# A three-block transformer in one kernel: 36 expert up groups moved under the choice and the spreading of the experts

## The reference

```python
q = (xt @ w_q).reshape(T, H, 256)
s1 = einsum('thd,hkd->thk', q[..., :128], keys1); s2 = einsum('thd,hkd->thk', q[..., 128:], keys2)
v1, i1 = top_k(s1, 16); v2, i2 = top_k(s2, 16)
cand = v1[..., :, None] + v2[..., None, :]          # 16 x 16 sums
sv, pos = top_k(cand, 16); eidx = take(i1 * 128 + i2, pos); gw = softmax(sv)
act = einsum('td,thkd->thk', xc, u_tab[eidx])
hact = gelu(act) * gc
return einsum('thk,thkd->td', hact, v_tab[eidx])
```

## Time and profile before

| | us |
|---|---|
| median of three runs (lowest, highest) | 3381.91 (3381.36, 3394.42) |
| profiled execution, its own time | 3379.55 |
| its span | 3377.8 |
| PE, DVE, ACT, POOL busy | 3076.7, 2061.3, 1342.0, 20.9 |
| PE idle before the transposes of the choice | 67.3 |

### The profile page before, as it was taken

One profiled execution on the slowest core, in us unless ns is written; L12 is line 12 of the kernel. 1 busy time (PEld: TensorE's weight loads), 2 busy tenths in 40 slices (PEclk: granted clock), 3 DMA queues, 4 the chain that ended last, 5 costly groups with the idle time before them and its releaser, 6 DMA issues.

```text
span 3377.8 us, 53195 instructions
## 1 busy us (share of the span) xinstructions
PE 3076.7 (91%) x19008; PEld 2712.4 (80%) x19008; DVE 2061.3 (61%) x3619; ACT 1342.0 (40%) x1953; POOL 20.9 (1%) x41
## 2 busy tenths in 40 slices
PE   8997699998999999999999898798926899999999
PEld 8986476898998798988898668784725799999998
DVE  5563543656557556567555636863599766666666
ACT  4332422444443434443444323331318644444443
POOL 0000000000000000000000000000000000000000
PEclk9999899999999999999999868898968999999999
DMA  7556143555554655554555314233410355555554
GB/s 246 186 161 188 56 162 119 174 184 201 184 183 131 219 185 186 184 172 143 198 184 189 124 54 140 90 100 113 155 44 0 101 187 186 187 187 188 187 187 157
DMA packets 141255, 525.50 MB, mean 156 GB/s; under 512 B 16154, under 2 KB 16154, under 8 KB 138320
## 3 DMA queue, kind: packets, MB, share of 16 engines
q1 hardware_dynamic: 134768, 490.79, 44.4%
q0 software_dynamic: 5520, 30.97, 2.8%
q10 hardware_dynamic: 848, 2.10, 0.2%
HBM read 520.65 MB, written 3.15 MB: 155 GB/s over the span
## 4 chain that ended last, share of the span: by engine, by line
PE 81%; DVE 12%; ACT 3%; DMA 2%; issue 2%; ACTq 0%; SPq 0%; DVEq 0%
PE psum L487 74%; PE psum L1464 2%; DMA ring<-wstream 2%; DVE wpair L458 1%; ACT small L1835 1%; DVE arena L2340 1%; PE psum L1033 1%; PE psum L611 1%; PE psum L1056 1%; ACT hpair L1839 1%; PE psum L1045 1%; PE psum L1449 0%; DVE xpair L666 0%; DVE arena L2540 0%; DVE arena L2454 0%
## 5 line engine op out<-in xcount | busy, mean ns | idle before, releaser
L487 PEld LDWEIGHTS psum<-xpair,wpair 128*128 128x128 f32 x11712 | 1461.7, 194 | 78.0 <-DVE wpair L458 41.0
L487 PE MATMUL psum<-xpair,wpair 128*128 128x256 f32 x11712 | 1475.5, 286 | 50.4 <-DVE wpair L458 38.2
L458 DVE TENSOR_TENSOR wpair<-ring,wpair 128x1024 fp32r<-128x1024 f32 (+1 forms) x872 | 1060.5, 1220 | 664.9 <-ACT wpair L455 662.6
L455 ACT CAST wpair<-ring 128x1024 fp32r<-128x1024 f32 (+1 forms) x872 | 908.1, 1044 | 1045.8 <-PE psum L487 913.9
L487 PE MATMUL psum<-wpair,hpair 128*128 128x512 f32 x3120 | 757.1, 391 | 3.4 <-DVE hpair L819 3.2
L487 PEld LDWEIGHTS psum<-wpair,hpair 128*128 128x128 f32 x3120 | 569.2, 188 | 113.8 <-issue 6.0
L487 PE MATMUL psum<-wpair,xpair 128*128 128x512 f32 (+3 forms) x1536 | 353.0, 391 | 15.6 <-DVE wpair L458 12.2
L487 PEld LDWEIGHTS psum<-wpair,xpair 128*128 128x128 f32 x1536 | 290.0, 195 | 76.9 <-DVE wpair L458 9.8
L796 ACT ACTIVATE small<-psum 128x256 f32<-128x256 f32 x260 | 99.9, 384 | 456.6 <-PE psum L487 456.6
L815 DVE TENSOR_TENSOR small<-small,arena 128x256 f32<-128x256 f32 x128 | 81.4, 636 | 141.6 <-ACT small L796 141.6
L611 PE MATMUL psum<-kc,arena 128*128 128x128 f32 (+1 forms) x212 | 44.2, 374 | 122.2 <-DVEq L2550 67.3
(11 more groups left out here) (305 smaller groups left out, 1617.1 us busy)
## 6 DMA issues: line engine op xcount, KB each, us to landing
ring<-wstream SPq DMA_DIRECT2D x934, 512.0 KB, 3.4
arena<-rows POOLq DMA_DIRECT2D x18, 1024.0 KB, 5.7
arena<-diag POOLq DMA_DIRECT2D x2, 1728.0 KB, 10.3
tbuf<-arena POOLq DMA_DIRECT2D x1, 2048.0 KB, 44.7
arena<-tbuf POOLq DMA_DIRECT2D x2, 1024.0 KB, 9.4
arena<-x_feat ACTq DMA_DIRECT2D x4, 256.0 KB, 8.7
res<-x_tok ACTq DMA_DIRECT2D x1, 1024.0 KB, 10.9
arena<-mem_feat POOLq DMA_DIRECT2D x1, 1024.0 KB, 5.0
```

The source lines that it names most:

```text
L455: eng.copy(hi, raw).then_inc(S("w_hi"), 1)
L458: eng.tensor_tensor(wpair[:, 1, o % PAIRS, 0:w], raw, hi.bitcast(F32), ALU.subtract)\
L487: mm = pe.matmul(out_, a[i], b[j], start=start and n == 0, stop=stop_ and last)
```

## The change

The first 24 up groups (`NA`) stand between the scores and the choice's transposes: PE makes them while DVE chooses, ACT puts their GELUs into `ga`, room taken from `wexp`. Pool makes the low halves of slots 0 to 25 of the expert stage; DVE makes none of them, and in the projection it no longer runs two slots ahead (`more=0`). Twelve more up groups (`NB`) stand in the spreading, one after every fifth round, with GELUs into a new tile `gb`, casts on ACT and halves on DVE in it. In every round DVE multiplies the 24 kept blocks' part straight from PSUM (`w_mul`), and then ACT copies the other 104 columns. The spreading is written out, not looped.

The expert blocks that are left run as 36 rounds of three (the up group of a new block, the down group of a new one and that of a kept one), then 54 rounds of two as before, and the last ones. The hidden tiles get a number of their own h, apart from the block f. ACT and DVE make the halves of round k + 1 in turn k. The stream is packed in the new order, and the scratch of the transfers that Pool issues is set to 4096 bytes, which makes room for `gb`. The feed-forward stages keep their code, with the number of slots a block written as 3.

```diff
+NA, NB = 24, 12
+N0 = NA + NB
+
+
+def peer_up(f):
+
+    return f if f <= N0 else N0 + 1 + 3 * (f - N0 - 1) if f <= 2 * N0 else 4 * N0 + 1 + 2 * (f - 2 * N0 - 1)
+
+
+def peer_down(f):
+    if f < N0:
+        return N0 + 1 + 3 * f + 2
+    if f < 2 * N0:
+        return N0 + 1 + 3 * (f - N0) + 1
+    return 2 * NKEY - 1 if f == NKEY - 1 else 4 * N0 + 1 + 2 * (f - 2 * N0) + 1
...
+        def pe_peer_up(pe, f, i=0, step=0):
+
+            s = STAGES["peer"]
+            pe.wait_ge(S("hid_act"), H0 + f - 1 + step * i)
+            slot = s.slot + peer_up(f)
+            w = weights(pe, slot, i)
+            for k in range(KD):
+                x_part(pe, k)
+                products(pe, psum[:, 4 + f % 2, 0:SEQ], part(w, slice(k * P, (k + 1) * P)),
+                         [xpair[:, a, k, :] for a in (0, 1)], k == 0, k == KD - 1,
+                         "hid_done" if k == KD - 1 else None)
+            hold(slot)
...
+        def pe_peer_down(pe, h, f, i=0, step=0):
+
+            s = STAGES["peer"]
+            slot = s.slot + peer_down(f)
+            w = weights(pe, slot, i)
+            pe.wait_ge(S("hid_out"), H0 + h + 1 + step * i)
+            for nn in range(2):
+                for t in range(NT):
+                    products(pe, bank(s.tile + nn, t), [hpair[:, a, h % 2, tt(t)] for a in (0, 1)],
+                             part(w, slice(nn * HALF, (nn + 1) * HALF)), h == 0, False,
+                             "down_done" if nn + t == 2 else None)
+            hold(slot)
+
+        def pe_peer(pe):
+
+
+            def round3(k, i=0):
+                pe_peer_up(pe, N0 + 1 + k, i, 4)
+                pe_peer_down(pe, 2 * k, N0 + k, i, 8)
+                pe_peer_down(pe, 2 * k + 1, k, i, 8)
+
+            def round2(f, i=0):
+                pe_peer_up(pe, f + 1, i, 6)
+                pe_peer_down(pe, f, f, i, 6)
+
+            pe_peer_up(pe, N0)
+            for k in range(4):
+                round3(k)
+            with pe.Fori(0, N0 // 4 - 2) as i:
+                for k in range(4, 8):
+                    round3(k, i)
+            for k in range(N0 - 4, N0):
+                round3(k)
+            with pe.Fori(0, (NKEY - 2 - 2 * N0) // 6) as i:
+                for f in range(2 * N0, 2 * N0 + 6):
+                    round2(f, i)
+            pe_peer_up(pe, NKEY - 1)
...
+        def act_peer(act, split):
+
+            o = ORDER[STAGES["peer"].slot][1]
+
+            def gelu(f, read, i=0, step=0):
+                act.wait_ge(S("hid_done"), H0 + f + 1 + step * i)
+                if read is not None:
+                    act.wait_ge(S("hid_out"), read)
+                act.activation(gated(f), psum[:, 4 + f % 2, 0:SEQ], ACT.Gelu).then_inc(S("hid_act"), 1)
+
+            def round3(k, i=0, slots=3):
+                gelu(N0 + k, H0 + 2 * (k - 2) + 1 + 8 * i if k >= 2 else None, i, 4)
+                for j in range(slots):
+                    split.one(o + N0 + 4 + 3 * k + j, i)
+
+            def round2(f, i=0, slots=2):
+                gelu(f, H0 + 2 * (f - N0 - 2) + 1 if f < 2 * N0 + 2 else H0 + f - 1 + 6 * i, i, 6)
+                for j in range(slots):
+                    split.one(o + 4 * N0 + 1 + 2 * (f + 1 - 2 * N0) + j, i)
...
+            def fresh_tile(k, h, i, wi, hi, step):
+
+                f = N0 + k
+                dve.wait_ge(S("hid_act"), H0 + f + 1 + step * i)
+                if h >= 2:
+                    dve.wait_ge(S("down_done"), D0 + h - 1 + hi * i)
+                dve.tensor_tensor(whole(h), gated(f), weight(f + step * i), ALU.mult).then_inc(S("hid_whole"), 1)
+                dve.wait_ge(S("hid_whole"), whole_count(k) + wi * i)
+                dve_halves(dve, h, whole(h), H0 + h + 1 + hi * i)
+
+            def early_tile(k, i, wi):
+
+                h = 2 * k + 1
+                if h >= 2:
+                    dve.wait_ge(S("down_done"), D0 + h - 1 + 8 * i)
+                if k < NA:
+                    src = ga[:, bass.ds(k + 4 * i, 1), :].rearrange("p o s -> p (o s)")
                 else:
-                    other = weight(f + i)
-                h = f0 + f
-                dve.tensor_tensor(whole(h), gated(h), other, ALU.mult).then_inc(S("hid_whole"), 1)
-                dve.wait_ge(S("hid_whole"), h + 1 + i)
-                dve.tensor_copy(hpair[:, 0, h % 2, :], whole(h)).then_inc(S("hid_hi"), 1)
-                dve.wait_ge(S("hid_hi"), h + 1 + i)
-                dve.tensor_tensor(hpair[:, 1, h % 2, :], whole(h), hpair[:, 0, h % 2, :].bitcast(F32), ALU.subtract)\
-                   .then_inc(S("hid_out"), 1)
-
-            loop_tiles(dve, split, name, per, step)
+                    src = whole(h)
+                    g = gb[:, bass.ds(k - NA + 4 * i, 1), :].rearrange("p o s -> p (o s)")
+                    dve.tensor_tensor(src, g, weight(k + 4 * i), ALU.mult).then_inc(S("hid_whole"), 1)
+                    dve.wait_ge(S("hid_whole"), whole_count(k) + 1 + wi * i)
+                dve_halves(dve, h, src, H0 + h + 1 + 8 * i)
...
+            def round3(k, i=0, slots=3):
+                wi = 4 if k < NA else 8
+                fresh_tile(k, 2 * k, i, wi, 8, 4)
+                early_tile(k, i, wi)
+                for j in range(slots):
+                    split.one(o + N0 + 4 + 3 * k + j, i)
...
-        wexp = region(0, SEQ, NKEY)
+        wexp = region(0, SEQ, NKEY - NA)
+        ga = region(SEQ * (NKEY - NA), NA, SEQ)
...
+            split.at = ORDER[STAGES["peer"].slot][1]
+            pool.wait_ge(S("w_lo"), split.at)
+            split.to(split.at + NA + 2)
...
+            for f in range(NA):
+                pe_peer_up(pe, f)
             pe.wait_ge(S("selected"), 1)
             pe_transpose(pe, "peer", [[sel[:, a, t, :] for a in (0, 1) for t in range(NT)],
                                       [sel[:, 2, t, :] for t in range(NT)]])
-
-            def spread(n, nr, first=False):
-
-                pe.wait_ge(S("oh_ready"), nr + 1)
-                pe.wait_ge(S("oh_act"), nr + 1)
-                if not first:
-                    pe.wait_ge(S("w_out"), nr - 3)
+            wait_lin(pe, STAGES["peer"].tile)
+            for n in range(SEQ // 4):
+                pe.wait_ge(S("oh_ready"), n + 1)
+                pe.wait_ge(S("oh_act"), n + 1)
+                if n >= 4:
+                    pe.wait_ge(S("w_out"), n - 3)
                 for j in range(4):
                     mm = pe.matmul(psum[:, n % 4, j * P:(j + 1) * P], oh1[:, n % 2, j, :],
                                    oh2[:, n % 2, j, :].bitcast(F32), start=True, stop=True)
+                    if j == 0:
+                        release(mm)
                 mm.then_inc(S("w_done"), 1)
-
-            wait_lin(pe, STAGES["peer"].tile)
-            for n in range(4):
-                spread(n, n, True)
-            with pe.Fori(1, SEQ // 16) as i:
-                for n in range(4):
-                    spread(n, i * 4 + n)
+                if n % 5 == 4 and n // 5 < NB:
+                    pe_peer_up(pe, NA + n // 5)
             pe.wait_ge(S("w_out"), SEQ // 4)
-            pe_ffn(pe, "peer", peer=True)
+            pe_peer(pe)
...
+            def early(f):
+                act.wait_ge(S("hid_done"), H0 + f + 1)
+                to = ga[:, f, :] if f < NA else gb[:, f - NA, :]
+                act.activation(to, psum[:, 4 + f % 2, 0:SEQ], ACT.Gelu).then_inc(S("hid_act"), 1)
+
+            split.to(o + 3)
+            for f in range(NA):
+                early(f)
+                split.to(o + min(f + 4, NA + 2))
+                if f == 17:
+                    act.wait_ge(S("top_shift"), 1)
+                    act.activation(cv[:, :, :, :].rearrange("p t h k -> p (t h k)"),
+                                   cv[:, :, :, :].rearrange("p t h k -> p (t h k)"), ACT.Exp).then_inc(S("top_exp"), 1)
...
+            for n in range(SEQ // 4):
+                act.wait_ge(S("w_mul"), n + 1)
+                act.copy(wexp[:, 4 * n:4 * n + 4, :], psum[:, n % 4, :].rearrange("p (s e) -> p s e", s=4)[:, :, NA:])\
+                   .then_inc(S("w_out"), 1)
+                if n + 2 < SEQ // 4:
+                    onehot(n + 2)
+                if n % 5 == 1 and n > 5:
+                    early(NA + n // 5 - 1)
+                if n % 5 == 2 and n // 5 < NB:
+                    split.to(o + NA + 3 + n // 5)
+            act_peer(act, split)
...
-                    split.cover("pq", n)
+                    split.cover("pq", n, more=0)
...
+            o = ORDER[STAGES["peer"].slot][1]
+            dve.wait_ge(S("w_lo"), o + NA + 2)
+            split.at = o + NA + 2
+            onehots(0)
+            onehots(1)
+            dve.wait_ge(S("hid_act"), H0 + NA)
+            for n in range(SEQ // 4):
+                g = ga[:, :, 4 * n:4 * n + 4]
+                dve.wait_ge(S("w_done"), n + 1)
+                dve.tensor_tensor(g, g, psum[:, n % 4, :].rearrange("p (s e) -> p e s", s=4)[:, 0:NA, :], ALU.mult)\
+                   .then_inc(S("w_mul"), 1)
```

(34 more changed lines are left out.)

176 lines of the change are left out of this document (91 added, 85 removed).

## The result

The changed kernel took 3397.32 us (median of 15 runs, 3387.43 to 3407.36) against 3385.53 us (15 runs, 3374.74 to 3403.52) for the kernel before: the ratio is 1.0028, 95% interval 1.0017 to 1.0040, or 9.5 us more (the two medians are 11.8 us apart). That is within 0.5% and inside the range of 3352 to 3408 us, but on the other side of the -2.6 us forecast. The profiled execution took 3398.31 us, its span is 3396.5 us, 18.7 more than before.

The account below looks back on a forecast made before the run. Three bounds follow each other: DVE in the choice, ACT in the spreading, PE in the expert blocks. From 3379.55 us, +12.4 + 17 + 31 - 63.0 = -2.6 gave 3377 us, range 3352 to 3408.

Parts of the forecast that it names:

- part 5: Choice of experts: Pool's halves hold up DVE's two-input instructions, between nothing and 35 us; 17 us taken.
- the two signs of failure: Prediction fails if PE's wait in the rounds of three is missing, or Pool's subtraction is slower than 2.88 us.
- rival B: Choice: DVE and Pool take full turns, +35 us instead of 17, 3395 us in all; chance 0.25.
- Part 4: Choice: 24 up groups take 69.1 us, Pool's half of 2.7 us is hidden, transposes start 12.4 us later.
- Rival E: Choice: Pool's half takes over 2.88 us and sets the up groups' pace; 3399 to 3427 us, chance 0.10.
- Part 3: Query projection: without DVE's lead of two slots, the third top-16 begins 10.5 us later.
- Part 6: Spreading: 12 up groups aren't hidden, five rounds take 10.7 us where they took 8.2; 31 us more.
- Parts 1 and 2: Expert blocks: 36 up groups leave, 103.7 us less, but PE waits 1.13 us in 36 rounds, 40.7; net 63.0 less.
- Rival D: Expert blocks: rounds of three don't wait, 40.7 us less, 3335 us in all; chance 0.05.
- The sum: Whole kernel: 12.4 + 17 + 31 - 63.0 = -2.6 us against the profiled execution's 3379.55 us.

Follow-up runs that it names:

- The edit in pieces: Changed kernel with each of the spreading's up groups cut into pieces of 6, 6, 6, 3 and 3 products, one behind each round; 3388.16 us in one run.
- Four edits of a few lines: Changed kernel plus halves one slot later in rounds of three, spreading's up groups in pieces, rank tables in PSUM, projection lead restored; together 3315.05 us, ratio 0.9780 to before.
- the last kernel: Changed kernel with all four edits, and 28 up groups in the choice and 8 in the spreading instead of 24 and 12; 3313.57 us, ratio 0.9772 to before.

## Why the prediction came out as it did

The step that failed is part 5, the size of the hold-up of DVE by Pool. Neither of the two signs of failure that the prediction named appeared: the wait in the rounds of three is there, and Pool's subtraction takes less than 2.88 us.

- **Part 5.** I took 17 us, the middle between nothing and 35, for want of a nearer row. It is 27.7 us. The mechanism is the one of rival B, and no in-between one: in the rows above an operation either takes its own time or waits for Pool's to end. B's 35 was too much: it gave DVE about one operation with two inputs in each of Pool's slots. Pool's subtraction took 2.45 us and not 2.7, which leaves a gap of about 0.48 us in each slot for one or two DVE operations, and five more operations passed in the 1.85 us in which Pool waited for ACT (its one Exp had a table load before and one behind it, 1.28 us each, at 2549.65 and 2551.38). B was too little in kind: I counted only operations with two inputs, and four casts, copies and scalar operations, 8.0 of the 27.7 us, were held as well. The middle of two mechanisms was a number that neither gives.
- The Trainium skill (SBUF — State Buffer, Who interferes with whom) states both halves: a DVE instruction with two SBUF inputs excludes a Pool instruction that reads SBUF, not one that only writes it, and copy, cast and tensor_scalar exclude Pool's where they run in a two-port mode. The traces agree: 16.37 us for sixteen picks beside subtractions, 5.46 beside memsets, 5.39 with one input in PSUM; 2.50 us for the cast at line 2704 (in which mode it ran no trace shows). With the estimate from the Trainium skill for Pool the prediction had 3388 us for B, a hold-up of 28. That it lies so near 27.7 is in part luck: it counted operations with two inputs alone, and those make 19.7.
- **Part 4, Pool's half.** 2.7 us taken, 2.452 measured (26 times, 63.6 us), under 2.88: the up groups run without a gap and end at 2565.71, which is 2555.8 without the 9.88 us from before; predicted 2555.4. Rival E is out. The estimate of 2.3 us from the Trainium skill (GPSIMD Engine Reference, 3.1 Elementwise — side-by-side cycle accounting) is 6% low; half of its 4497 ns is 2.25 us, 8% low.
- **Part 3.** +10.5 predicted, +11.25 measured, as the part described it: PE waits 2.01, 3.88 and 3.88 us, and the top-16s start 20.3 us apart (2454.66, 2475.00, 2495.33), 20.15 predicted.
- **Part 6.** +31 predicted, +27.85 measured; five rounds 10.33 us for 10.7. No table load came with a GELU in the spreading. The edit in pieces bears out the cause that the part named, that a whole group isn't hidden.
- **Parts 1 and 2.** -63.0 predicted, -57.98 measured. The wait is there, with the chain as written: 4.04 us for 4.12. But a round lost 1.30 us, not 1.13, and so 46.9 us, not 40.7: 4.04 is 1.16 more than the up group's 2.88, and the next up group starts 5.58 us behind the first down group (2851.21, 2856.79), where it is 5.46 without the wait (2846.61, 2852.07). Without the wait the blocks are 104.9 us shorter than before, for 103.7 predicted. The multiply at a step of 104 took 0.66 us, just beyond the slow end of the bounds (0.42 to 0.64). Rival D is out (3377 - 40.7 is 3336, not the 3335 written there).
- **The sum** by the measured terms is 11.25 + 27.70 + 27.85 - 57.98 = +8.8 us in place of -2.6 (in the prediction, 12.4 + 17 for the first two, measured 38.95, +9.6). Part 5 alone is 10.7 us off, and the other errors, +0.75, -3.2 and +5.0, with 2 us less where the forecast let PE be last, nearly cancel. The 9.88 us from ahead of the change belong to the two profiled executions; the ratio of the runs, +9.5 us, leaves little room for them. Rival B's 3395 us stands close to the median of 3397.32 by luck: it is +15.4 us on its base, and the runs show +9.5.

So against the 104.9 us that left the expert blocks stand 113.7: 46.9 for a wait in the rounds of three, 27.85 in the spreading, 27.7 for Pool's turns in the choice, 11.25 for the lost lead. Four edits of a few lines take back 46.9, 14.4, 9.8 and 12.9 of it, and the change with them is 2.2% (1.9 to 2.5) faster than the kernel before.

## What to carry to other kernels

Before you hand work to Pool, list what DVE does meanwhile by operands: here an operation with two SBUF inputs waited for the end of each Pool instruction that read, and a copy, cast or scalar operation from SBUF to SBUF also for one that only wrote; a reduction, a MAX8, an operation with one of its two inputs in PSUM, or a copy into PSUM did not wait. When a bound lies between two mechanisms, price each and choose one; their middle is the time of neither. Where slots are counted in rounds, look whose buffer the round's last slot needs: one slot's shift in the order was worth 46.9 us here, more than all that Pool cost.

## What the runs showed of the hardware

- A Pool subtraction of 128x1024 (fp32 in, fp32r out) took 2.45 us on average and DVE's own 1.23; a Pool memset of the same size 0.954 us. Per element Pool's memsets of one and eight elements had pointed to 4.2 us for 1024.
- A cast of 128x256 from SBUF to SBUF took 0.29 us alone and a copy of that size into PSUM 0.42; the first is held by Pool, the second isn't. Of the two, the faster one was held.
- The 22 reductions of 128x4096 took 7.00 to 7.01 us the 14 times that no product of PE ran beside them; 7.59 to 7.69 the five times that up groups ran beside the whole of them, with Pool subtracting, with Pool writing, and with Pool doing nothing; and 7.32 to 7.46 the three times that up groups ran beside a part. So it isn't Pool that makes the difference. Which of PE, ACT's casts and the loads, all at work together there, makes them 8% to 10% longer is open.
- In the projection of the changed kernel the granted clock was 0.66 from 2457.70 to 2462.10 and 0.50 from 2478 to 2483, each time behind a wait of PE of 3.88 us; 24 products took 4.34 us in the first, and 3.13 where it was 1.00. Little or nothing was lost by it, since PE then had to wait for DVE's next half in any case (1.01 us from 2462.05 on).
- The granted clock of a stretch of attention that no edit touches lay anywhere from 0.50 to 0.83 between executions, and the projection behind it began anywhere within 15.7 us (2415.20 to 2430.88). One profile against another says nothing on 10 us of such a span; the stages, seam to seam, agreed within 0.5 us where nothing was changed in them, but for the spreading (135.45 to 136.45) and the projection of the last kernel (1.4 us longer).
